# Latent mixers: eight of the twelve convolution units placed between the attention's heads, both norms moved to the mixer's end

## The reference, cut to what matters

```python
def hybrid_mixer(h, cos, sin, w_in, q_a_norm, w_uq, kv_a_norm, w_ukv, conv_w, attn_out_norm, conv_out_norm, w_o):
    proj = h @ w_in
    c_q, c_kv, k_pe, gate_b, gate_c, val = jnp.split(proj, offs, axis=-1)
    q = (rms_norm(c_q, q_a_norm) @ w_uq).reshape(B, S, N_HEADS, QK_NOPE_DIM + QK_ROPE_DIM)
    ...
    kv = (rms_norm(c_kv, kv_a_norm) @ w_ukv).reshape(B, S, N_HEADS, QK_NOPE_DIM + V_HEAD_DIM)
    ...
    attn = causal_attention(q_full, k_full, v).reshape(B, S, ATTN_WIDTH)
    conv = gate_b * causal_short_conv(gate_c * val, conv_w)
    merged = jnp.concatenate([rms_norm(attn, attn_out_norm), rms_norm(conv, conv_out_norm)], axis=-1)
    return merged @ w_o
```

## Time and profile before

| | |
|---|---|
| median of three runs | 3444.86 us (3434.57 to 3447.27) |
| profiled execution, its own time | 3430.56 us |
| its span in the profile | 3428.8 us |
| TensorE (PE) busy | 3254.8 us, 95% |
| PE weight loads | 2593.2 us, 76% |
| VectorE (DVE) busy | 1818.3 us, 53% |
| ScalarE (ACT) busy | 1182.4 us, 34% |
| GpSimd (POOL) busy | 975.9 us, 28% |
| mean granted TensorE clock | 0.971 of full |

### The profile page before, as it was taken

How to read it: one execution, slowest core, us unless ns; L and a number is a source line. 1 busy time by engine, 2 the same in 40 slices (tenths; PEclk the granted TensorE clock), 3 DMA queues, 4 the chain that set the end, 5 groups by cost and what they waited for, 6 DMA issues and landing times.

```text
span 3428.8 us, 40302 instructions
## 1 busy us (share of the span) xinstructions
PE 3254.8 (95%) x14517; PEld 2593.2 (76%) x14517; DVE 1818.3 (53%) x2459; ACT 1182.4 (34%) x1780; POOL 975.9 (28%) x675
## 2 busy tenths in 40 slices
PE   6999999999999999999899997999999999889998
PEld 4888876678887888775688886767777777778887
DVE  6454455555545533546655434446777675375443
ACT  3222243532223222335422223454333231343332
POOL 2993000069903800000089600000895000021000
PEclk7999999999999999999999998999999998899999
DMA  6664352156634633331266533112664344143332
GB/s 211 208 206 132 92 136 60 37 172 208 194 95 141 189 98 90 89 94 37 64 214 208 154 97 104 50 44 85 198 206 139 96 119 82 51 126 101 96 94 86
DMA packets 576559, 420.30 MB, mean 123 GB/s; under 512 B 28715, under 2 KB 535962, under 8 KB 575302
## 3 DMA queue, kind: packets, MB, share of 16 engines
q1 hardware_dynamic: 537330, 286.09, 28.3%
q0 software_dynamic: 33952, 122.70, 11.8%
q10 hardware_dynamic: 5172, 10.17, 1.0%
HBM read 413.10 MB, written 8.68 MB: 123 GB/s over the span
## 4 chain that ended last, share of the span: by engine, by line
PE 82%; DVE 11%; ACT 4%; issue 2%; DMA 1%; ACTq 0%; SPq 0%; DVEq 0%
PE bank L325 24%; PE bank L326 24%; PE bank L327 24%; PE bank L1322 2%; DVE tmp L450 2%; PE bank L1350 2%; DVE w_lo L306 2%; DVE h_lo L460 1%; PE bank L1336 1%; DVE folded L510 1%; PE bank L431 1%; DVE w_lo L297 1%; PE bank L409 1%; ACT w_hi L280 1%; PE bank L2395 1%
## 5 line engine op out<-in xcount | busy, mean ns | idle before, releaser
L325 PE MATMUL bank<-h_hi,w_hi 128*128 128x512 f32 x2656 | 1056.2, 398 | 55.6 <-DVE h_lo L460 20.8
L326 PE MATMUL bank<-h_lo,w_hi 128*128 128x512 f32 x2656 | 1043.6, 393 | 0.0
L327 PE MATMUL bank<-h_hi,w_lo 128*128 128x512 f32 x2656 | 1043.4, 393 | 0.0
L306 DVE TENSOR_TENSOR w_lo<-raw,w_hi 128x1024 fp32r<-128x1024 f32 x438 | 659.0, 1505 | 579.1 <-ACT w_hi L289 577.0
L289 ACT ACTIVATE w_hi<-raw 128x1024 fp32r<-128x1024 f32 x438 | 462.1, 1055 | 650.8 <-PE bank L327 650.8
L325 PEld LDWEIGHTS bank<-h_hi,w_hi 128*128 128x128 f32 x2656 | 503.3, 189 | 192.2 <-DVE h_lo L460 37.6
L327 PEld LDWEIGHTS bank<-h_hi,w_lo 128*128 128x128 f32 x2656 | 503.0, 189 | 108.8
L326 PEld LDWEIGHTS bank<-h_lo,w_hi 128*128 128x128 f32 x2656 | 503.8, 190 | 102.6 <-issue 0.5
L693 POOL TENSOR_TENSOR mod_acc<-mod_acc,mod_w 128x1024 f32<-128x1024 f32 x168 | 430.2, 2561 | 14.0
L325 PE MATMUL bank<-hid_hi,w_hi 128*128 128x512 f32 x1056 | 412.3, 390 | 4.9 <-DVE w_lo L306 4.4
L327 PE MATMUL bank<-hid_hi,w_lo 128*128 128x512 f32 x1056 | 410.9, 389 | 0.0
(11 more groups left out here) (348 smaller groups left out, 3229.9 us busy)
## 6 DMA issues: line engine op xcount, KB each, us to landing
raw<-in_ffn_w_gu SPq DMA_DIRECT2D x176, 512.0 KB, 4.3
mod_w<-in_w_ada POOLq DMA_DIRECT2D x128, 512.0 KB, 3.8
mod_w<-in_mod_w POOLq DMA_DIRECT2D x96, 512.0 KB, 4.1
raw<-in_ffn_w_in SPq DMA_DIRECT2D x88, 512.0 KB, 3.7
raw<-in_ffn_w_down SPq DMA_DIRECT2D x64, 512.0 KB, 3.5
raw<-in_w_in SPq DMA_DIRECT2D x34, 512.0 KB, 3.6
raw<-in_ffn_w_out SPq DMA_DIRECT2D x32, 512.0 KB, 3.5
raw<-in_ffn_w_down SPq DMA_DIRECT2D x32, 384.0 KB, 3.0
```

The source lines that it names most:

```text
L306: loop(nc.vector.tensor_tensor(w_lo[:, u % 2, :], raw[:, u % 2, :], w_hi[:, u % 2, :].bitcast(F32), ALU.subtract), "split_lo", times)
L325: nc.tensor.matmul(dst, a_hi, b_hi, start=start, stop=False)
L326: nc.tensor.matmul(dst, a_hi, b_lo, start=False, stop=False)
L327: return nc.tensor.matmul(dst, a_lo, b_hi, start=False, stop=stop)
```

## The change

`FRONT = 10`: only ten of the eighteen column units (0 to 9) run at the start. The other eight (10 to 17) run inside the attention, one behind each head, all in bank 1; their weights are loaded after those of queries, keys and values. `attend_pe`, `attend_act` and `attend_dve` are gone; their loops are written out in the mixer. On TensorE a head is now: turn, scores of the next head, values, unit. The first scores come before the values' unit, whose banks are now 1 and 7. The convolution keeps its own sum of squares in a new buffer `c_sq` of two halves, which `conv_sum` sums with eight small matmuls. The attention's sum and spread stand inside the last unit; the convolution's stand in the output projection, whose first two columns are interleaved (`begin`). The key-value norm is scaled and split behind the first query unit. An Exp on one value is placed before the key copies. Code that is moved unchanged is left out of the diff.

```diff
@@ pe_out
-        def pe_out(pe, key, kts, b_hi, b_lo, ready, last=False, order=None):
+        def pe_out(pe, key, kts, b_hi, b_lo, ready, last=False, begin=None):
...
+                if begin is not None and isinstance(i, int) and i == 0:
+                    begin(pe)
+                    return
@@ new buffer and helpers
+        c_sq = place("c_sq", [P, 2, S], F32, [mod_at])
+        FRONT = 10
+        def conv_square(act, key, t):
+            wait(act, "conv_ready", (key, t))
+            if t >= 2:
+                wait(act, "conv_added", (key, t - 1))
+            done(nc.scalar.activation(c_sq[:, min(t, 1), :], conv[:, t, :], ACT.Square, scale=S ** -0.5), "conv_squared",
+                 (key, t))
+        def conv_add(dve, key, t):
+            wait(dve, "conv_squared", (key, t))
...
+            done(nc.vector.tensor_tensor(c_sq[:, 0, :], c_sq[:, 0, :], c_sq[:, 1, :], ALU.add), "conv_added", (key, t))
+        def conv_sum(pe, key, bank):
+            wait(pe, "conv_added", (key, 2))
+            wait(pe, "conv_squared", (key, 3))
+            for t in range(TQ):
+                for half in range(2):
+                    ins = nc.tensor.matmul(psum[bank][:, t:t + 1], c_sq[:, half, t * P:(t + 1) * P], ones[:, 0:1],
+                                           start=half == 0, stop=half == 1, skip_group_check=True)
+            done(ins, "conv_sum", key)
@@ sp_mla
-            for n, (c, m) in enumerate(mla_units()):
+            for n in range(FRONT):
...
+            for a, b in UQ_HEADS:
+                load(sp, wq[:, :, a * HD:b * HD], 3 * (b - a) * HD, pattern="p (kt n) -> p kt n", n=(b - a) * HD)
+                if a == 0:
                     wait(sp, "kpe_ready", key)
                     src = work[0:ROPE, 0, :]
                     for h in range(HEADS):
                         done(sp.dma_start(k_full[NOPE:HD, h, :], src), "kpe_spread", key, 16)
...
+            for n in range(FRONT, len(mla_units())):
+                unit(n)
             sp_out(sp, d["w_o"][l], KT)
@@ pe_mla, behind the key pairs
+            wait(pe, "kpe_spread", key)
+            wait(pe, "query_turned", (key, HEADS - 1))
+            wait(pe, "key_read", (key, 0))
+            pe_scores(pe, key, jobs, 0)
+            wait(pe, "key_read", (key, 3))
             s = unit_ready(pe)
...
             wait(pe, "value_read", (key, 3))
+            for h in range(HEADS):
+                pe_turn(pe, key, jobs, h)
+                if h + 1 < HEADS:
+                    pe_scores(pe, key, jobs, h + 1)
+                pe_values(pe, key, jobs, h)
+                n = FRONT + h
+                if h:
+                    wait(pe, *bank_reader(key, n - 1))
+                s = unit_ready(pe)
+                for kt in range(KT):
+                    c = slice(kt * P, (kt + 1) * P)
+                    ins = mm3(psum[1][:, :], w_hi[:, s, c], w_lo[:, s, c], h_hi[:, kt, :], h_lo[:, kt, :], kt == 0,
+                              kt == KT - 1)
+                    if h == HEADS - 1 and kt == 4:
+                        norm_sum(pe, (key, "attn"), 3)
+                    if h == HEADS - 1 and kt == 6:
+                        norm_spread(pe, (key, "attn"), 3)
+                unit_end(ins)
...
+            def begin(pe):
+                conv_sum(pe, key, 4)
+                for mm, kts in ((0, range(4)), (1, range(4)), (0, (4,)), (1, (4,)), (0, (5,)), (1, (5,)), (0, (6,)),
+                                (1, (6,)), (0, (7,)), (1, (7,))):
+                    s = (u0 + mm) % 2
+                    pe.wait_ge(sg.sem("split_lo"), u0 + mm + 1)
+                    for kt in kts:
+                        wait(pe, "norm_lo", ((key, "attn"), kt) if kt < 4 else ((key, "conv"), kt - 4))
+                        c = slice(kt * P, (kt + 1) * P)
+                        ins = mm3(psum[5 + mm][:, :], w_hi[:, s, c], w_lo[:, s, c], b_hi(kt), b_lo(kt), kt == 0, kt == KT - 1)
+                        if mm == 0 and kt == 1:
+                            conv_spread(pe, key, 4)
+                        if kt == KT - 1:
+                            done(ins, "unit_used")
@@ act_mla
+            nc.scalar.activation(misc[:, 7:8], eps[:, :], ACT.Exp)
             for pair in range(4):
...
             split_hi(act)
+            act_exps(act, key, jobs, 0)
             split_hi(act)
+            for h in range(HEADS):
+                n = FRONT + h - 1
+                if h and n % 3 == 0:
...
+                    done(nc.scalar.activation(work[:, 1, :], psum[1][:, :], ACT.Copy), "proj_read", (key, n))
+                act_turned(act, key, jobs, h)
+                if h:
+                    split_hi(act)
+                if h + 1 < HEADS:
+                    act_exps(act, key, jobs, h + 1)
...
             norm_root(act, (key, "attn"), 3)
+            round_attn(0)
+            conv_square(act, key, 3)
+            round_attn(1)
+            conv_root(act, key, 4)
+            split_hi(act)
+            round_attn(2)
+            round_attn(3)
+            norm_round(act, (key, "conv"), 4, None, lambda m: c_hi[:, m, :])
             act_out(act, key, KT, key == final)
@@ dve_mla
             split_lo(dve)
+            dve_scores(dve, key, jobs, 0)
+            value(0)
+            value(1)
+            dve_divide(dve, key, jobs, 0)
+            value(2)
+            value(3)
             split_lo(dve)
+            for h in range(HEADS):
+                if h:
+                    conv_take(dve, key, FRONT + h - 1, v0 + h)
+                if h + 1 < HEADS:
+                    dve_scores(dve, key, jobs, h + 1)
+                if h:
+                    split_lo(dve)
+                if h + 1 < HEADS:
+                    dve_divide(dve, key, jobs, h + 1)
...
             add_square(dve, (key, "attn"))
             norm_invert(dve, (key, "attn"))
+            scale(0)
+            conv_take(dve, key, FRONT + HEADS - 1, v0 + HEADS)
+            scale(1)
+            low(0)
+            conv_invert(dve, key)
+            split_lo(dve)
+            low(1)
+            scale(2)
+            scale(3)
+            low(2)
+            low(3)
+            wait(dve, "norm_lo", ((key, "attn"), 3))
+            norm_scale_split(dve, (key, "conv"), 4, 4, lambda m: conv[:, m, :], lambda m: col(("conv_out_norm", l), m), None,
+                             lambda m: c_lo[m // 2][:, m % 2, :], lambda m: c_hi[:, m, :])
```

More of the change, by code:

```diff
@@ L890, in body @@
                             pe.wait_ge(sg.sem("x_ready"), i * 2 + (x0 + mm - 1))
-                        for n, kt in enumerate(order or range(a, b)):
+                        for kt in range(a, b):
                             ready(pe, kt)
@@ L1488, in early, with mla_jobs @@
                     half = raw[:, turn.sp % 2, 0:S].rearrange("p (h c) -> p h c", c=NOPE)
-                    done(sp.dma_start(half, w[part, 0]), "ukv_loaded", (key, part), 16)
-                load(sp, w[part, 1], S, first=S, early=early, pattern="p (h c) -> p h c", c=NOPE)
+                    done(sp.dma_start(half, wkv[part, 0]), "ukv_loaded", (key, part), 16)
+                load(sp, wkv[part, 1], S, first=S, early=early, pattern="p (h c) -> p h c", c=NOPE)
+            for n in range(FRONT, len(mla_units())):
+                unit(n)
             sp_out(sp, d["w_o"][l], KT)
-        def mla_jobs():
+        def mla_jobs(key):
             jobs = []
@@ new lines, in conv_take @@
+        def conv_take(dve, key, n, u):
+            l = 0 if key[1] == 1 else 1
+            t, part = divmod(n - CONV0, 3)
+            bank = n % 2 if n < FRONT else 1
+            if part == 1:
+                wait(dve, "proj_read", (key, n - 1))
+                dve.wait_ge(sg.sem("unit_used"), u)
+                done(nc.vector.tensor_tensor(conv_u[:, :], work[:, 1, :], psum[bank][:, :], ALU.mult), "conv_in", (key, t))
+                dve.wait_ge(sg.sem("conv_in"), sg.count["conv_in"])
+                taps = [col(("conv_w", l), 4 * j + t) for j in range(3)]
+                y = conv[:, t, :]
+                vstep(nc.vector.tensor_scalar(y, conv_u[:, :], taps[2], None, ALU.mult))
+                vstep(nc.vector.scalar_tensor_tensor(y[:, 1:], conv_u[:, 0:S - 1], taps[1], y[:, 1:], ALU.mult, ALU.add))
+                vstep(nc.vector.scalar_tensor_tensor(y[:, 2:], conv_u[:, 0:S - 2], taps[0], y[:, 2:], ALU.mult, ALU.add))
+            if part == 2:
+                dve.wait_ge(sg.sem("unit_used"), u)
+                y = conv[:, t, :]
+                done(nc.vector.tensor_tensor(y, y, psum[bank][:, :], ALU.mult), "conv_ready", (key, t))
@@ L1683, in beside @@
-            def beside(act, j):
-                if j < 4:
-                    wait(act, "norm_scaled", ((key, "conv"), j))
-                    done(nc.scalar.activation(c_hi[:, j, :], tmp[:, j % 3, :], ACT.Identity), "norm_hi",
-                         ((key, "conv"), j))
-            wait(act, "norm_spread", (key, "conv"))
```

(6 more changed lines are left out.)

178 lines of the change are left out of this document (66 added, 112 removed).

## The result

The changed kernel takes 3452.43 us (median of seven runs, 3448.15 to 3453.82), against 3434.79 us for the kernel before (median of seven, the three shown above among them). The ratio is 1.0043, with a 95% interval of 1.0027 to 1.0058: slower by a little under the 0.5% that was called the limit, and not by chance. The time lies inside the predicted range, but only because the first three runs of before stood high. What counts is the move: forecast -0.9 us, found +17.6 by the medians, and 15 (9 to 20) by the ratio.

The account below looks back on a forecast made before the run. TensorE, 82% of the chain of waits, was taken as the bound. Terms of 31.7 + 10.6 + 80.4 + 11.0 + 23.35 made 157.1 us per mixer; clock -6.1 + 5.2 gave -0.9, so 3444.0 us, range 3427 to 3457.

Parts of the forecast that it names:

- Queries and keys: Mixer from head 1's queries to the values: 31.7 us against 30.36, with norm, copies and their wait costed at nothing.
- values and first softmax: From the values to head 0's turn: 10.6 us against 17.5 before, including 2.8 us of new holes.
- a head (seven of them): Heads 0 to 6, turn, scores, values and unit: 11.5 us each, 80.4 in all, no hole, 2.2 us VectorE slack.
- head 7: Last head with its unit and the attention norm's sums and spread: 11.0 us, most of the norm's wait gone.
- tail, with the low clock in it: From the last unit's end to the third output unit: 23.35 us, plus 0.9 for low clock before the last hole.
- the stretch: One mixer, unit 10's first matmul to the third output unit's: 157.1 us at full clock, against 156.95 before.
- second attention tile: In the tail: TensorE idles 2.8 us because both splits stand ahead of this tile's low part.
- third output unit: In the tail: TensorE waits 4.3 us, as interleaved columns free this unit's weights only when the first column ends.
- The table load: Exponential's table loaded ahead of the keys: 1.28 us, costed at nothing; a drain would put the forecast 2 us higher.
- The clock: First mixer regains 6.4 us; both mixers lose 1.7 for the 4.3 us hole and 0.9 ahead: plus 5.2.
- The rival "VectorE becomes the bound": Between heads, the division's chain runs over 2.2 us longer than counted and delays the turns: 3463.6 us, chance 0.08.
- The rival of the hidden tail: Tail waits of 2.8 and 4.3 us hidden in both mixers, no clock lost: 3424.6 us, chance 0.12.

Follow-up runs that it names:

- The two kernels with the copies elsewhere: Changed kernel with the eight key copies behind the last query weights on SyncE's queue, 3434.01 us; or issued by GpSimd at the same moment, 3437.82 us.
- the kernel with the copies last: Changed kernel with the wait for rotated keys and their eight copies behind the last query weights in SyncE's queue instead of the first; 3434.01 us, ratio 0.9996.
- the last three kernels: Changed kernel, copies behind the last query weights, plus attention tiles ahead of the split: 3430.53 us; first output column finished first: 3425.63; both: 3424.55.
- The kernel before with its copies moved: Kernel before the change, wait and eight copies two units earlier, behind the load of unit 10 instead of unit 12; 3458.04 us, ratio 1.0073.

## Why the prediction was wrong, point by point

**The step that failed** is the last but one of "Queries and keys": the copies "now stand ahead of the loads of the second and third query weights. Those are split two units before they are used, so some 11 us of units cover them; cost nothing." It measured 16.2 us. Two things were wrong in it. The wait and the copies had no duration there, though the wait held the queue for 10.1 us after the load's slot was free, and the eight issues for 5.05 more. And the cover was counted up to the use of the weights on TensorE. What counts is the split's place in ScalarE's list: the wait for the load is in front of it, and the copies of finished query heads are queued behind it. The first of these has only 2.3 us to spare behind the split (0.9 of idle ScalarE and 1.4 before the swap, in the kernel with the copies from GpSimd), not 11 us. With the 7.5 us ahead of the split 9.8 us were covered, and the load came 15.2 us late. The two kernels with the copies elsewhere show it as cause, the first by place, the second by queue; how it divides between the wait and the issues is worked out from rows and was not run.

**What held**, with the term first and then the kernel with the copies last, second mixer, where nothing is in the way (from the rows above and the start of its queries, 1492.84; seven heads took 78.6; a unit's end is the start of its last matmul and 0.23, as the prediction counts, so head 7 ends at 1624.31, and holes are distances from there, up to 0.2 more than the brackets):

| term | predicted | measured |
|---|---|---|
| queries and keys | 31.7 | 31.4 |
| values and first softmax | 10.6 | 10.5 |
| a head (seven of them) | 11.5 | 11.23 |
| head 7 | 11.0 | 11.0 |
| tail, with the low clock in it | 23.35 + 0.9 | 24.0 |
| the stretch | 158.0 | 155.4 |
| in the tail: wait for the convolution's sums | 1.85 | 1.7 |
| those sums, eight | 1.7 | 1.8 |
| second attention tile | 2.8 | 1.9 |
| third output unit | 4.3 | 4.3 |

The heads follow each other without a hole, here and in the changed kernel, and the key-value norm and the squares cost nothing, as costed. Of the 2.6 us by which the stretch is shorter than forecast, 1.8 are the seven heads. The wait at the second attention tile was oversized by 0.9 us, of which the tail gives back only 0.3: its sparse part runs at a lower clock than the 0.9 us allowed for (0.56 over the 7 us from 1627). The steps that the prediction lists for the tail also make 18.45 to the end of the second column (7.15, fifteen of 0.69, a spread of 0.95), not the 19.05 written; the 0.6 has no term.

**The table load** was costed at nothing, too. ScalarE's timeline in the changed kernel, first mixer:

```profile
524.79 1.28 ACT L1726 ACT_TABLE_LOAD   x1
526.09 0.20 ACT L1726 ACTIVATE misc<-eps 128x1 f32<-128x1 f32 x1
526.66 1.20 ACT L1730 ACTIVATE k_full<-bank 64x512 f32<-64x512 f32 x2 [0.37 <-PE bank L327]
```

The exponential starts 0.02 us after the load, and the first key copies still wait for TensorE. The drain of 1.4 us behind a load, which the Trainium skill gives (ScalarE: Activation LUTs, "What ACT_TABLE_LOAD costs"), and the 2 us that it would have cost here, did not come.

**The clock.** The prediction gave back 6.4 us in the first mixer and took 1.7 behind each 4.3 us hole and 0.9 ahead of it. With the copies last the first mixer's stretch is 155.4 us as well, so the 6.4 did come back, and behind the 4.15 us hole the clock was 0.61 in the first mixer and 0.57 in the second, the value of the earlier trace rows, which costs the 1.7. In the changed kernel the new holes took the gain away: 0.96 in the first mixer's stretch, and 5.4 us for the two low stretches behind them.

**The total.** Without the failed step the forecast would read -0.9, and the kernel without it measured 0.9996, -1.4 us with 4 us to either side. That the two agree so well is in part luck: its two stretches make 310.8 us in its profile where the forecast had 316.0, and its later phases were longer than before's (last paragraph of this section). The rival "VectorE becomes the bound" ended on the right side by the wrong mechanism. The rival of the hidden tail did not come by itself, but its waits could be cut: that is what the last three kernels do.

**The rest of the difference.** The profiled executions lie 20.3 us apart, of which the two stretches explain 9.1 (329.4 against 320.3). 3.4 more are the low clock behind the third output unit's hole, which lies outside the stretch. The other 7.8 are in phases whose instructions did not change, 6.0 of them behind the second mixer. They don't belong to the failed step: the kernel with the copies last has 7.5 of them as well, as its stretches are 9.5 us shorter than before's and its span is 1.4 longer. The kernel before with its copies moved, whose later phases are those of before, has 13.0 behind the second mixer. The execution of before that was profiled is 4.2 us under its median, and the runs of one kernel lie up to 22 us apart; so it looks like an execution that was short in those phases. I take it for that, and have not shown it.

## What to carry to other kernels

A DMA issue is an instruction with a duration on its queue: when a wait and eight small copies move ahead of a load, add up how long the wait lasts, their issue time and the load's time to land, and then ask what stands behind the *consumer* of that load in its own in-order engine, not when the data is used. A few small copies that are needed late go last in the queue of the weights, or to a queue that is idle. And interleaving two output columns to cover a late operand takes the cover from the third: the first weights' slot comes free later, so finish one column as soon as its operands allow.

## What the runs showed of the hardware

- Eight copies of 64 KB (32 partitions of 512 floats) took 5.05 us to issue on SyncE's queue, 0.63 each, and 4.00 us, 0.5 each, on GpSimd's; a single load of weights took SyncE's queue 0.37 alone, and 0.54 to 0.72 close behind another.
- A low clock followed every 4 to 5.5 us hole of TensorE that I looked at (0.50 to 0.66 over the next 4 to 7 us), and one of four holes of 2.12 us. So a wait of 5.4 us cost 8.
- The eight sums of f32 columns took 1.92 us at full clock (first mixer of the changed kernel) and 3.14 us in its second, where the clock was 0.57, just where the chain of the norm hangs on them.
